# Block-product FFN: modulation columns shifted by half a step, first block step reordered

## The chip, the cores and the metric

The kernel runs on one core of a Trainium2 chip. The metric is the device time of one execution in microseconds. A core has TensorE (PE), VectorE (DVE), ScalarE (ACT) and GpSimd (POOL), which run their own instruction streams and meet at semaphores; SyncE (SP) issues all DMA transfers, in one queue.

## The reference

The program is a two-layer trunk on 1024 latent tokens of 1024 channels and a context of 256. Layer 0 has a recurrent mixer, layer 1 a pooling mixer; each is followed by a gated feed-forward block, and every sub-layer is normalised, modulated and gated by six vectors per layer, computed from the condition `c`.

```python
mod_l = jnp.split((sc @ ada_w[i] + ada_b[i])[:, None, :], N_MOD, axis=-1)   # sc = silu(c)
...
def _conv_ffn(h, w_up, conv_w, conv_b, w_down):
    z = h @ w_up.astype(h.dtype)
    u, v = z[..., :D_FF], z[..., D_FF:]
    u = _dwconv(u, conv_w, conv_b, (FFN_CONV // 2, FFN_CONV // 2))   # width 3 along the tokens
    return (jax.nn.gelu(u) * v) @ w_down.astype(h.dtype)
```

## The kernel before

Everything is channel-major: 8 tiles of 128 channels (KT), tokens along the free dimension, in two halves of 512. A float32 product is made of three fp32r products: each operand is split into a rounded part `_hi` (ScalarE, a copy) and a rest `_lo` (GpSimd or VectorE, a subtraction), and hi*hi, hi*lo and lo*hi are summed in PSUM.

**A feed-forward block** (`ffn(L)` on each engine, L = 0 and 1) has 24 steps j (FJ), one for each 128 of the 3072 hidden channels. Step 0 is made as two plain products (`first_pair`, weights "A" and "B") while the input arrives. From step 1 the up projection of u and v (two outputs, two token halves, eight channel tiles) is made of seven "quarters" of 12 products each, in the order 11, 12, S4, S1, S2, S3, 22 (`quarter`), a block scheme with fewer products than the eight plain ones. On the weight side S1, S2, S3 and S4 are combinations of weight halves, made by GpSimd (`combine`, L1317), rounded by ScalarE (`round_op`, L882) and completed by GpSimd (`lo_of_op`, L1330, So_lo, WA_lo and WB_lo). On the token side the operands are sums and differences of the halves of the input, T_raw[0] to T_raw[3], made once a block by VectorE (`right_raws`), rounded by ScalarE (`round_t`) and completed by VectorE (`right_lo`) and, for the last, GpSimd. S1 reads T[0], S2 T[1], S3 T[2] and 22 T[3]; 11, 12 and S4 read the input itself.

VectorE turns the quarters into Ub (u, by adds L1854, L1866, L1869) and V (L1863 and L1871 make U2, then L1873, L1877). ScalarE and VectorE do the convolution (`tap` L1055, `taps` L1815 and L1820), ScalarE GeLU (L1060), VectorE the gating S[1] = S[0] * V (`gated`, L1832), ScalarE F_hi (L1094), GpSimd F_lo (L1350). The down projection (`down`, L461, 8 tiles m, 48 products, weights "C" with WC_lo L1187) of step j-1 follows the quarters of step j; VectorE adds each tile to Y (`add_down`, L1744; the first time a copy, L1742). Tiles of `down` take turns on three bank pairs (4, 0, 6). Steps 2 to 22 are a hardware loop; step 23 and the last down product (`down_last`) are written out, with the sums of squares of the next norm among its adds.

**Modulation columns.** The columns of layer 1 are made beside block 0. Each step handles units e = 2j and 2j+1: a 512 KB weight unit is loaded to E (`load_unit`; one buffer, so a load waits until the sum before it is done), GpSimd multiplies it with silu(c) (`ada_product`, L1222), VectorE sums over the channel tiles (`ada_sum`, L1479), TensorE sums over partitions with products of one column (`ada_columns`, L494), VectorE adds the bias (`add_ada_bias`, L1502). Units 0 and 1 are loaded at the end of the out-projection's loads; their products come before the next stream on GpSimd and their sums in the first step of the block. In a step both sums come ahead of the U2 add, the columns after 22 and the bias add behind the taps; tile m = 1 of `down` waits for that add, since it writes bank 0, where the columns are.

**Order.** The order on each engine is written out by hand; every wait is for the semaphores named in the code. In the first step of a block TensorE does all seven quarters, then down(0).

Of the kernel before, what the change touches and what calls it, by code (L numbers as in the profile page):

```python
# [23 lines left out]
KT = D // P  # L24
# [44 lines left out]
def build_trunk(nc, xT, ctxT, params, ada, wA, wB, wC, gatew, poolw, poolcnt, ident_in, outT):  # L69
    with ExitStack() as top:  # L70
# [91 lines left out]
        READY_FIRST = ("S1", "11", "12", "S4", "S2", "S3", "22")  # L162
# [145 lines left out]
        def _(sp_):  # L308
# [147 lines left out]
        def _(pe):  # L456
# [183 lines left out]
            def down(L, j):  # L640
# [5 lines left out]
                for m in range(KT):  # L646
                    if m < 2:
                        if not first:
                            pe.wait_ge(d_added, 8 * c + m - 1)
                        if m == 1 and L == 0:  # L650
                            pe.wait_ge(ada_added, NH + 3 + j)
# [4 lines left out]
                    b = (4, 0, 6)[m % 3]  # L656
# [3 lines left out]
            def down_last(L):  # L660
# [29 lines left out]

# [23 lines left out]
            def ffn_step(L, j):  # L714
# [13 lines left out]
                quarter("S2", t, first)  # L728
                if first and L == 0:
                    pe.wait_ge(u_evac, 1)  # L730
# [4 lines left out]
                pe.wait_ge(up_added, added_at("u0", t))  # L735
                quarter("S3", t, first)
                pe.wait_ge(up_added, added_at("u2", t))
                quarter("22", t, first)
                if L == 0:
                    if first:  # L740
                        pe.wait_ge(ada_added, NH + 2)
                    else:
# [104 lines left out]
        def _(act):  # L847
# [220 lines left out]
            def ffn_first(L):  # L1068

                round_t(L, 0)  # L1070
                round_op("S1", L, 1)
                round_op("11", L, 1)
                round_op("12", L, 1)
# [5 lines left out]
                round_op("S4", L, 1)  # L1079
                round_t(L, 2)  # L1080
                round_t(L, 1)
                round_op("S2", L, 1)
                round_op("S3", L, 1)
                round_op("22", L, 1)
                round_t(L, 3)
                copy_p1(UP * L + 1)
                gelu(L, 0)

            def ffn_step(L, j):
# [3 lines left out]
                act.wait_ge(f_mul, t)  # L1093
                A(F_hi[:], S[1][:], ACT.Copy).then_inc(f_hi, 1)  # L1094
                if not first:
                    copy_p1(t)
                if not (first and L == 0):
                    round_down(L, j - 1)
# [77 lines left out]
            norm_root(5, 1)  # L1176
            next_stream(5, 2, lambda h: fill_ffn(1, h))
# [3 lines left out]
        def _(pool):  # L1181
# [51 lines left out]

            def next_stream(q, i, lo):
# [12 lines left out]
                if lo:  # L1247
                    lo(1)
# [52 lines left out]
            def combine(name, L, j):  # L1301


                t, n = UP * L + j, N_STD + FJ * L + j
                A1, A2, B1, B2 = (raw[s][:, hs(h)] for s in "AB" for h in range(2))
                S1_, S2_, S4_ = (So_raw[:, i * HF:i * HF + HF] for i in range(3))
                dst, a, b, op, before = {
                    "S1": (S1_, B1, B2, ALU.add, None), "S2": (S2_, S1_, A1, ALU.subtract, "S1"),
                    "S3": (B1, A1, B1, ALU.subtract, "S1"), "S4": (S4_, A2, S2_, ALU.subtract, "S2")}[name]
                if before is None:  # L1310
                    pool.wait_ge(raw_full["B"], 16 * n + 16)
                    pool.wait_ge(raw_full["A"], 16 * n + 16)
                else:
                    pool.wait_ge(made, made_at(before, t))
                if name != "S3" and not (isinstance(t, int) and t == 1):
                    pool.wait_ge(op_done, done_at(name, t - 1))
                TT(dst, a, b, op).then_inc(made, 1)  # L1317
# [14 lines left out]
            def ffn_first(L):  # L1332

                for name in ("S1", "S2", "S3", "S4"):
                    combine(name, L, 1)
                for name in ("S1", "11", "12", "S4", "S2", "S3", "22"):
                    lo_of_op(name, L, 1)
                for k in range(KT // 2):
# [4 lines left out]
            def ffn_step(L, j):  # L1343
                t = UP * L + j
                static = isinstance(j, int)
                first, last = static and j == 1, static and j == FJ - 1
                if L == 0:
                    ada_product(2 * j)
                pool.wait_ge(f_hi, t)
                TT((F_lo_last if last else F_lo)[:], S[1][:], F_hi[:].bitcast(F32), ALU.subtract)\  # L1350
                    .then_inc(f_ready, 1)
                if not (first and L == 0):
                    lo_of_unit("C", t - 1)
                if last:
                    if L == 0:
# [647 lines left out]
```

## Time and profile before

| | us |
|---|---|
| median of 3 runs | 2371.55 (2368.89 to 2373.41) |
| the profiled execution, its own time | 2371.26 |
| its span, first to last instruction | 2369.5 |
| mean granted TensorE clock | 0.946 |
| block 0, steps 3 to 22 (20 steps) | 728.14 |
| block 1, steps 2 to 22 (21 steps) | 646.12 |

In the trace, times are microseconds from the span's start. A product of 512 columns starts 0.23 us after the one before it when TensorE runs freely; its own duration is longer, since products are pipelined. The granted clock is a share of 2.4 GHz.

### The profile page before, as it was taken

To read this page: it belongs to the slowest core of one execution; us is meant where nothing else is said; L and a number is where in the kernel's file an instruction comes from. 1 tells how busy PE (TensorE), PEld (TensorE's weight loads), DVE (VectorE), ACT (ScalarE), POOL (GpSimd) and SP (SyncE) were. 2 spreads that over 40 slices of the span, in tenths; PEclk is the share of its full clock that TensorE was granted. 3 is DMA by queue.
4 is the path that set the end of the run, shared out by engine and by line. 5 is a ranking of instruction groups with operands and counts; after the bars stand their busy time and mean duration, and the time that the engine had idled before them with its cause. 6 is when DMAs were issued, how large, how long until landed. Compare 5 with 4: busy or idle time off the path is not lost.

```text
span 2369.5 us, 26733 instructions
## 1 busy us (share of the span) xinstructions
PE 2113.4 (89%) x9040; PEld 1692.5 (71%) x9040; DVE 1545.9 (65%) x1535; ACT 812.2 (34%) x1072; POOL 1342.9 (57%) x836
## 2 busy tenths in 40 slices
PE   7899997955889899899898997967999999999996
PEld 7677775844667677677676776855888888888885
DVE  6688885188656656656656568488665555556667
ACT  3557655244222222222222234453222222222222
POOL 1423323366575766765756736257666666666663
PEclk9999998967999999999999997978999999999998
DMA  6133221221222122222121240021111111111113
GB/s 261 71 104 110 77 101 71 80 98 36 73 69 78 63 71 80 69 73 79 63 80 62 71 151 27 19 80 45 53 45 53 44 53 53 48 50 53 53 44 142
DMA packets 52120, 174.91 MB, mean 74 GB/s; under 512 B 4817, under 2 KB 5105, under 8 KB 50929
## 3 DMA queue, kind: packets, MB, share of 16 engines
q1 hardware_dynamic: 52080, 174.41, 21.0%
q8 instruction: 22, 0.36, 0.1%
q14 instruction: 18, 0.14, 0.0%
HBM read 161.80 MB, written 12.58 MB: 74 GB/s over the span
## 4 chain that ended last, share of the span: by engine, by line
PE 48%; issue 18%; POOL 15%; DVE 10%; ACT 7%; DMA 2%; POOLq 0%; SPq 0%; ACTq 0%; DVEq 0%
PE ps L461 21%; PE ps L709 18%; PE ps L593 3%; POOL F_lo L1350 2%; POOL WC_lo L1187 2%; POOL E L1222 2%; POOL WA_lo L1330 2%; POOL So_raw L1317 2%; POOL So_lo L1330 2%; DMA E<-ada 2%; DVE T_lo L1809 1%; PE ps L821 1%; POOL WB_lo L1330 1%; DVE V L1439 1%; PE ps L500 1%
## 5 line engine op out<-in xcount | busy, mean ns | idle before, releaser
L1744 DVE TENSOR_TENSOR Y<-Y,ps 128x1024 f32<-128x1024 f32 x336 | 401.4, 1217 | 45.8 <-PE ps L461 24.2
L461 PE MATMUL ps<-F_hi,WC_hi 128*128 128x512 f32 x736 | 242.7, 408 | 39.7 <-DVE M L1502 36.1
L1330 POOL TENSOR_TENSOR So_lo<-So_raw,So_hi 128x512 fp32r<-128x512 f32 x138 | 262.8, 1930 | 11.4 <-ACT So_hi L882 11.4
L1479 DVE TENSOR_REDUCE red<-E 128x128 f32<-128x1024 f32 x47 | 92.9, 1977 | 250.9 <-POOL E L1222 250.9
L1222 POOL TENSOR_TENSOR E<-E,silu_c 128x1024 f32<-128x1024 f32 x47 | 89.6, 1906 | 281.1 <-DMA E<-ada 281.1
L461 PE MATMUL ps<-F_hi,WC_lo 128*128 128x512 f32 x736 | 233.8, 396 | 0.0
L461 PE MATMUL ps<-F_lo,WC_hi 128*128 128x512 f32 x704 | 222.2, 397 | 0.0
L882 ACT ACTIVATE So_hi<-So_raw 128x512 fp32r<-128x512 f32 x138 | 81.6, 620 | 393.5 <-POOL So_raw L1317 393.5
L1094 ACT ACTIVATE F_hi<-S 128x1024 fp32r<-128x1024 f32 x46 | 48.8, 1060 | 464.8 <-DVE S L1832 454.2
L1350 POOL TENSOR_TENSOR F_lo<-S,F_hi 128x1024 fp32r<-128x1024 f32 x44 | 105.9, 2406 | 175.8 <-ACT F_hi L1094 175.8
L461 PEld LDWEIGHTS ps<-F_hi,WC_hi 128*128 128x128 f32 x736 | 137.0, 193 | 82.5 <-DVE M L1502 45.5
L461 PEld LDWEIGHTS ps<-F_hi,WC_lo 128*128 128x128 f32 x736 | 140.8, 191 | 31.1
L709 PE MATMUL ps<-H_hi,WA_hi 128*128 128x512 f32 x368 | 148.0, 402 | 11.3 <-POOL WA_lo L1330 11.3
L461 PEld LDWEIGHTS ps<-F_lo,WC_hi 128*128 128x128 f32 x704 | 135.1, 192 | 29.9
L709 PE MATMUL ps<-T_hi,So_hi 128*128 128x512 f32 x368 | 146.0, 397 | 1.7 <-DVE T_lo L1809 1.7
L709 PE MATMUL ps<-H_lo,WA_hi 128*128 128x512 f32 x368 | 147.4, 401 | 0.0
L709 PE MATMUL ps<-H_hi,WA_lo 128*128 128x512 f32 x368 | 147.2, 400 | 0.0
L709 PE MATMUL ps<-T_lo,So_hi 128*128 128x512 f32 x368 | 145.6, 396 | 0.0
L709 PE MATMUL ps<-T_hi,So_lo 128*128 128x512 f32 x368 | 145.5, 395 | 0.0
L1863 DVE TENSOR_TENSOR U<-t,ps 128x512 f32<-128x512 f32 x46 | 31.4, 683 | 169.6 <-PE ps L709 169.6
L709 PE MATMUL ps<-H_hi,WB_hi 128*128 128x512 f32 x184 | 80.4, 437 | 45.9 <-DVE U L1863 45.9
L1330 POOL TENSOR_TENSOR WA_lo<-rawA,WA_hi 128x512 fp32r<-128x512 f32 x92 | 118.9, 1314 | 0.0
(269 smaller groups left out, 5352.4 us busy)
## 6 DMA issues: line engine op xcount, KB each, us to landing
rawA<-wA SPq DMA_DIRECT2D x60, 512.0 KB, 3.3
rawB<-wB SPq DMA_DIRECT2D x60, 512.0 KB, 3.3
E<-ada SPq DMA_DIRECT2D x47, 512.0 KB, 3.8
rawC<-wC SPq DMA_DIRECT2D x46, 512.0 KB, 3.3
quad<-ada SPq DMA_DIRECT2D x8, 2048.0 KB, 9.5
ada_first<-ada SPq DMA_DIRECT2D x4, 2048.0 KB, 16.4
outT<-X SPq DMA_DIRECT2D x16, 512.0 KB, 2.8
X<-outT SPq DMA_DIRECT2D x16, 512.0 KB, 6.8
```

Of the source, the lines that this page charges most:

```text
L461: mm = pe.matmul(out, w[:, w_cols:w_cols + P], (hi, lo)[part], start=first and w is W_hi[s] and part == 0, stop=last and w is W_lo[s])
L593: mm = pe.matmul(out, gw[:, gi], src, start=True, stop=True)
L709: mm = pe.matmul(ps[:, OUT[name]], w[:, at + k * P:at + k * P + P], right[part][:, k], start=k == 0 and w is hi and part == 0, stop=k == K ...
L882: A(dst[:, at:at + HF], src[:, src_at:src_at + HF], ACT.Copy).then_inc(op_hi, 1)
L1094: A(F_hi[:], S[1][:], ACT.Copy).then_inc(f_hi, 1)
L1187: TT(W_lo[s][:], raw[s][:], W_hi[s][:].bitcast(F32), ALU.subtract).then_inc(w_ready[s], 1)
L1222: TT(dst[:], dst[:], silu_c[:, :, 0:1].to_broadcast([P, KT, P]), ALU.mult).then_inc(e_mul, 1)
L1317: TT(dst, a, b, op).then_inc(made, 1)
L1330: TT(lo[:, at:at + HF], src, hi[:, at:at + HF].bitcast(F32), ALU.subtract).then_inc(op_ready, 1)
L1350: TT((F_lo_last if last else F_lo)[:], S[1][:], F_hi[:].bitcast(F32), ALU.subtract)\
L1479: dve.tensor_reduce(red[:, i], src[:].rearrange("p k m -> p m k"), mybir.AxisListType.X, ALU.add)\
L1744: TT(Y[:, m], Y[:, m], flat(ps[:, b:b + 2, :]), ALU.add).then_inc(d_added, 1)
```

## The change

The columns' stages are shifted by half a step: the second sum of a pair is made at the start of the next step, TensorE makes the columns between 12 and S4 of that step, and the bias add follows the first Ub add. On GpSimd F_lo is put before the first column product and the combinations before the second. Units 0 and 1 are loaded, multiplied and summed in the out-projection; the last pair's second sum, columns and coefficients go into the last down product's adds. In the first step of both blocks the weight combinations are made earlier (in `next_stream`), S4 is completed first, and down(0) comes right after S4, on two bank pairs instead of three; VectorE does the taps and the gating of step 0 between the T_raw's. For block 1 the first down weight is completed before the stream that leads to the block.

```diff
-        READY_FIRST = ("S1", "11", "12", "S4", "S2", "S3", "22")
+        READY_FIRST = ("S4", "S1", "11", "12", "S2", "S3", "22")
@@ SyncE: the out-projection's loads
+                if i == 3:
+                    load_unit(0)
+                    load_unit(1)
                 load_raw("A", NH + 2 + i)
                 load_raw("B", NH + 2 + i)
-            load_unit(0)
-            load_unit(1)
@@ TensorE: down
-                        if m == 1 and L == 0:
-                            pe.wait_ge(ada_added, NH + 3 + j)
+                        if m == 1 and L == 0 and not first:
+                            pe.wait_ge(ada_added, NH + 2 + j)
+                    elif first:
+                        pe.wait_ge(d_added, 8 * c + m - 1)
...
-                    b = (4, 0, 6)[m % 3]
+                    b = (4, 0)[m % 2] if first else (4, 0, 6)[m % 3]
@@ TensorE: down_last
-                        pe.wait_ge(ada_added, NH + 1 + FJ)
+                        pe.wait_ge(ada_added, NH + FJ)
...
+                    if n == 7 and L == 0:
+                        ada_columns(4 * NH + 2 * FJ, 2, ps[:, 3, 0:2])
@@ TensorE: ffn_step
                 if not first:
+                    if L == 0:
+                        pe.wait_ge(d_added, 8 * (c - 1))
+                        pe.wait_ge(ada_added, NH + j)
+                        ada_columns(4 * NH + 2 * j, 2, ps[:, 0, 0:2])
                     pe.wait_ge(d_added, 8 * c - 10)
                 quarter("S4", t, first)
+                if first:
+                    down(L, 0)
                 quarter("S1", t, first)
...
-                        pe.wait_ge(d_added, 8 * (c - 1))
-                    ada_columns(4 * NH + 2 * j + 2, 2, ps[:, 0, 0:2])
-                if not last:
+                if not first and not last:
                     down(L, j - 1)
@@ ScalarE: ffn_first
-                round_t(L, 0)
+                round_op("S4", L, 1)
                 round_op("S1", L, 1)
                 round_op("11", L, 1)
-                round_op("12", L, 1)
                 A(Ub[:, 1:T + 1], flat(AB01), ACT.Copy).then_inc(u_evac, 1)
                 tap(L, 0)
-                round_op("S4", L, 1)
-                round_t(L, 2)
-                round_t(L, 1)
+                round_op("12", L, 1)
                 round_op("S2", L, 1)
+                round_t(L, 0)
                 round_op("S3", L, 1)
                 round_op("22", L, 1)
+                gelu(L, 0)
+                round_t(L, 2)
+                copy_p1(UP * L + 1)
+                act.wait_ge(f_mul, UP * L + 1)
+                A(F_hi[:], S[1][:], ACT.Copy).then_inc(f_hi, 1)
+                round_t(L, 1)
                 round_t(L, 3)
-                copy_p1(UP * L + 1)
-                gelu(L, 0)
@@ ScalarE, before the second block's stream
+            round_down(1, 0)
             next_stream(5, 2, lambda h: fill_ffn(1, h))
@@ GpSimd: next_stream
                 if lo:
+                    for name in MADE_ORDER:
+                        combine(name, q // 4, 1)
                     lo(1)
@@ GpSimd: the out-projection
             for m in range(KT):
+                if m == 6:
+                    ada_product(0)
                 lo_of_unit("AB"[m % 2], NH + m // 2 + 1)
+                if m == 6:
+                    ada_product(1)
@@ GpSimd: ffn_first and ffn_step
-                for name in ("S1", "S2", "S3", "S4"):
-                    combine(name, L, 1)
+                for name in READY_FIRST:
                     lo_of_op(name, L, 1)
+                pool.wait_ge(f_hi, UP * L + 1)
+                TT(F_lo[:], S[1][:], F_hi[:].bitcast(F32), ALU.subtract).then_inc(f_ready, 1)
...
+                if not first:
+                    pool.wait_ge(f_hi, t)
+                    TT((F_lo_last if last else F_lo)[:], ...).then_inc(f_ready, 1)
                 if L == 0:
                     ada_product(2 * j)
...
                 lo_of_op("12", L, j + 1)
+                for name in MADE_ORDER:
+                    combine(name, L, j + 1)
                 if L == 0:
                     ada_product(2 * j + 1)
-                for name in ("S1", "S2", "S3", "S4"):
-                    combine(name, L, j + 1)
@@ GpSimd, before the second block's stream
+            lo_of_unit("C", UP)
             next_stream(5, 2, lambda h: fill_ffn(1, h))
@@ VectorE: even_sums_whole (the out-projection's squares)
+                for i in range(2):
+                    ada_sum(0, i)
@@ VectorE: add_down_last
+                    if n == 3 and L == 0:
+                        ada_sum(FJ - 1, 1)
+                    if n == 9 and L == 0:
+                        later_coefs()
@@ VectorE: right_raws (T_raw[0], T_raw[2], T_raw[1], T_raw[3] in this order)
-                right_lo(L, 0)                       # was behind T_raw[0]
+                taps(L, 0)                           # behind T_raw[2]
+                gated(L, 0)                          # behind T_raw[1]
@@ VectorE: ffn_first
                 right_raws(L)
+                right_lo(L, 0)
+                add_down(L, 0)
                 right_lo(L, 1)
-                taps(L, 0)
                 right_lo(L, 2)
-                if L == 0:
-                    ada_sum(0, 0)
-                    ada_sum(0, 1)
@@ VectorE: ffn_step
-                gated(L, j - 1)
-                if L == 0 and not first:
-                    ada_sum(j, 0)
+                if not first:
+                    if L == 0:
+                        ada_sum(j - 1, 1)
+                    gated(L, j - 1)
                 TT(u_0, t1[:], p["12"], ALU.add).then_inc(up_added, 1)
...
+                if L == 0 and not first:
+                    add_ada_bias(ps[:, 0, 0:2], 46 + 2 * j, 2, NH + 1 + j)
+                    ada_sum(j, 0)
...
+                if first:
+                    v_first_half()
+                    taps(L, j)
+                    if L == 0:
+                        ...
+                        add_ada_bias(ps[:, 0, 0:2], 48, 2, NH + 2)
+                        ada_sum(1, 0)
+                    return
```

## Rows read from the trace of the kernel before

**Rows 1.** The page, busy time by engine (share of the span) and instructions.
```profile
PE 2113.4 (89%) x9040; PEld 1692.5 (71%) x9040; DVE 1545.9 (65%) x1535; ACT 812.2 (34%) x1072; POOL 1342.9 (57%) x836
```
**Rows 2.** Busy time by stretches, the loops: us; busy by engine; clock, DMA, GB/s.
```profile
647.89:1376.03 728.14, 653.64 (x2722) 518.81 (x2721) 454.75 (x421) 173.78 (x240) 483.81 (x300) 0.96 0.21 71
1653.20:2299.32 646.12, 646.12 (x2773) 518.95 (x2772) 394.14 (x379) 182.19 (x252) 433.11 (x273) 1.00 0.15 50
```
**Rows 3.** TensorE's waits from 647.9 to 1376: total us, times, longest.
```profile
PE ps L709 <- DVE U L1863: 41.8, 20, 2.7
PE ps L461 <- DVE M L1502: 32.7, 20, 2.3
```
**Rows 4.** Timeline of TensorE, the columns: start, us, what.
```profile
816.06 0.50 PE L494 MATMUL ps<-ones,red 128*128 128x1 f32 x4
```
**Rows 5.** Timeline of VectorE, a step of block 1.
```profile
2300.89 1.22 DVE L1832 TENSOR_TENSOR S<-S,V 128x1024 f32<-128x1024 f32 x1
2305.35 0.69 DVE L1854 TENSOR_TENSOR Ub<-t,ps 128x512 f32<-128x512 f32 x1 [3.24 <-PE ps L709]
2313.75 0.69 DVE L1863 TENSOR_TENSOR U<-t,ps 128x512 f32<-128x512 f32 x1 [7.71 <-PE ps L709]
```
**Rows 6.** Timeline of GpSimd and VectorE, a step of block 0.
```profile
799.57 1.91 POOL L1222 TENSOR_TENSOR E<-E,silu_c 128x1024 f32<-128x1024 f32 x1 [11.86 <-DMA E<-ada]
801.44 2.41 POOL L1350 TENSOR_TENSOR F_lo<-S,F_hi 128x1024 fp32r<-128x1024 f32 x1
806.15 2.55 POOL L1330 TENSOR_TENSOR WA_lo<-rawA,WA_hi 128x512 fp32r<-128x512 f32 x2
810.52 1.27 POOL L1317 TENSOR_TENSOR So_raw<-rawB 128x512 f32<-128x512 f32 x1
810.60 1.91 DVE L1479 TENSOR_REDUCE red<-E 128x128 f32<-128x1024 f32 x1 [6.45 <-POOL E L1222]
815.68 5.72 POOL L1330 TENSOR_TENSOR So_lo<-So_raw,So_hi 128x512 fp32r<-128x512 f32 x3
```
**Rows 7.** The page, a costly group (busy, mean ns) and transfers (us to landing).
```profile
L1094 ACT ACTIVATE F_hi<-S 128x1024 fp32r<-128x1024 f32 x46 | 48.8, 1060 | 464.8 <-DVE S L1832 454.2
...
E<-ada SPq DMA_DIRECT2D x47, 512.0 KB, 3.8
rawC<-wC SPq DMA_DIRECT2D x46, 512.0 KB, 3.3
```
**Rows 8.** Timeline of TensorE, first steps; in brackets the idle time before.
```profile
546.70 0.79 PE L709 MATMUL ps<-H_hi,WA_hi 128*128 128x512 f32 x1 [5.54 <-POOL WA_lo L1330]
...
598.31 0.99 PE L494 MATMUL ps<-ones,red 128*128 128x1 f32 x4 [10.62 <-DVE red L1479]
...
1602.36 0.77 PE L709 MATMUL ps<-H_hi,WA_hi 128*128 128x512 f32 x1 [5.75 <-POOL WA_lo L1330]
```
**Rows 9.** Timeline of VectorE, first step of block 0.
```profile
540.41 6.79 DVE L1809 TENSOR_TENSOR T_lo<-T_raw,T_hi 128x512 fp32r<-128x512 f32 x4
563.64 2.30 DVE L1815 SCALAR_TENSOR_TENSOR S<-Ub,par,S 128x1024 f32<-128x1024 f32 x1
602.10 1.23 DVE L1742 COPY Y<-ps 128x1024 f32<-128x1024 f32 x1 [2.61 <-PE ps L461]
```
**Rows 10.** Timeline of GpSimd, ahead of block 0.
```profile
480.90 1.90 POOL L1222 TENSOR_TENSOR E<-E,silu_c 128x1024 f32<-128x1024 f32 x1 [1.60 <-DMA E<-ada]
482.76 2.35 POOL L1222 TENSOR_TENSOR E_first<-E_first,silu_c 128x1024 f32<-128x1024 f32 x1
```
**Rows 11.** Timeline of SyncE and VectorE, ahead of block 1.
```profile
1539.09 0.33 SPq L446 DMA_DIRECT2D rawC<-wC  x1
1545.51 1.57 DVE L1439 TENSOR_TENSOR V<-V 128x512 f32<-128x512 f32 x1
1551.68 0.69 DVE L1445 TENSOR_TENSOR V<-V,acc 128x512 f32<-128x512 f32 x1
```
**Rows 12.** Timeline of TensorE, start of the last down product of block 0.
```profile
1399.13 0.50 PE L461 MATMUL ps<-F_hi,WC_hi 128*128 128x512 f32 x1 [1.02 <-DVE M L1502]
```

More of the change, by code:

```diff
@@ L1092, in ffn_step @@
                 first, last = static and j == 1, static and j == FJ - 1
-                act.wait_ge(f_mul, t)
-                A(F_hi[:], S[1][:], ACT.Copy).then_inc(f_hi, 1)
                 if not first:
+                    act.wait_ge(f_mul, t)
+                    A(F_hi[:], S[1][:], ACT.Copy).then_inc(f_hi, 1)
                     copy_p1(t)
-                if not (first and L == 0):
                     round_down(L, j - 1)
@@ L1232, in add_odd, with combine @@
                     TT(X[:, m, hs(h)], X[:, m, hs(h)], Y[:, m, hs(h)], ALU.add).then_inc(x_new[1], 1)
+            def combine(name, L, j):
+                t, n = UP * L + j, N_STD + FJ * L + j
+                A1, A2, B1, B2 = (raw[s][:, hs(h)] for s in "AB" for h in range(2))
+                S1_, S2_, S4_ = (So_raw[:, i * HF:i * HF + HF] for i in range(3))
+                dst, a, b, op, before = {
+                    "S1": (S1_, B1, B2, ALU.add, None), "S2": (S2_, S1_, A1, ALU.subtract, "S1"),
+                    "S3": (B1, A1, B1, ALU.subtract, "S1"), "S4": (S4_, A2, S2_, ALU.subtract, "S2")}[name]
+                if before is None:
+                    pool.wait_ge(raw_full["B"], 16 * n + 16)
+                    pool.wait_ge(raw_full["A"], 16 * n + 16)
+                else:
+                    pool.wait_ge(made, made_at(before, t))
+                if name != "S3" and not (isinstance(t, int) and t == 1):
+                    pool.wait_ge(op_done, done_at(name, t - 1))
+                TT(dst, a, b, op).then_inc(made, 1)
             def next_stream(q, i, lo):
@@ L1299, in _ @@
             lo_of_unit("C", 0)
[L1301 to L1317, printed above, removed]
             def lo_of_op(name, L, j):
@@ L1346, in ffn_step @@
                 first, last = static and j == 1, static and j == FJ - 1
+                if not first:
+                    pool.wait_ge(f_hi, t)
+                    TT((F_lo_last if last else F_lo)[:], S[1][:], F_hi[:].bitcast(F32), ALU.subtract)\
+                        .then_inc(f_ready, 1)
                 if L == 0:
                     ada_product(2 * j)
[L1349 to L1352, printed above, removed]
+                if not first:
                     lo_of_unit("C", t - 1)
                 if last:
-                    if L == 0:
-                        ada_product(2 * j + 1)
                     pool.wait_ge(lastw_hi, L + 1)
@@ L1739, in add_down @@
                     dve.wait_ge(d_done, 8 * (FJ * L + j) + m + 1)
-                    b = (4, 0, 6)[m % 3]
+                    b = (4, 0)[m % 2] if isinstance(j, int) and j == 0 else (4, 0, 6)[m % 3]
                     if isinstance(j, int) and j == 0:
@@ L1744, in add_down, with later_coefs @@
                         TT(Y[:, m], Y[:, m], flat(ps[:, b:b + 2, :]), ALU.add).then_inc(d_added, 1)
+            def later_coefs():
+                add_ada_bias(ps[:, 3, 0:2], 46 + 2 * FJ, 2, NH + 1 + FJ)
+                dve.wait_ge(ada_added, NH + 1 + FJ)
+                coefs(2, 1, 0)
+                coefs(3, 1, 1)
+                shift_steps(1)
+                gates(2, 1, 0)
+                gates(3, 1, 1).then_inc(coef_ready, 1)
+                dve.wait_ge(coef_ready, 3)
+                dve.wait_ge(cols_step, 1)
+                TS(cc[:, 2], cc[:, 1], ROUNDER, None, ALU.add).then_inc(cols_step, 1)
+                dve.wait_ge(cols_step, 2)
+                TS(cc[:, 0], cc[:, 2], -ROUNDER, -1.0, ALU.add, ALU.mult).then_inc(cols_ready, 1)
             def add_down_last(L):
@@ L1826, in gated @@
                 if isinstance(j, int) and j == 0:
-                    dve.wait_ge(unit_done["B"], N_STD + L + 1)
+                    for s in "AB":
+                        dve.wait_ge(unit_done[s], N_STD + L + 1)
                     TT(S[1][:], S[0][:], flat(AB45), ALU.mult).then_inc(f_mul, 1)
```

50 lines of the change are left out of this document (12 added, 38 removed).

## The prediction

> **What bounds the kernel now.** I read the page first: TensorE is busy for 89% of the span and nothing else passes 65% [rows 1]. So only stretches in which TensorE stands still or runs slowly can give time back. Second, the busy time by stretches, cut at the first product of a step [rows 2]. The two feed-forward blocks run the same 132 large products per step, and only the first also makes the modulation columns of the next layer. Its 20 steps from 647.89 to 1376.03 take 728.14 us, 36.41 each; the second block's 21 steps take 646.12 us, 30.77 each. The second has no TensorE idle time and a granted clock of 1.00 (2.4 GHz throughout), the first 0.96. Third, TensorE's waits in the first block's loop [rows 3]: 41.8 us before the product "22" for the add that makes U2, and 32.7 us before the down product for the add of the modulation bias. That is 3.73 us a step, for one small side computation. Its chain is: column unit by DMA, product on GpSimd (L1222), sum on VectorE (L1479), four one-column products (L494), bias add (L1502).
>
> Step excess: 36.41 - 30.77 = 5.64 us, of which 3.73 waiting and at most 0.50 for the four one-column products, a row of whose group lasts 0.50 us [rows 4]; I take 0.36, since they overlap their neighbours. The rest, 1.55 us, is the clock: stretches at 1.2 GHz follow some of the waits.
>
> **The loop after the change (first block, steps 3 to 22).** The second sum of a pair moves to the start of the next VectorE step, the columns go between "12" and "S4", the bias add follows the first Ub add, and on GpSimd F_lo comes before the first product and the combinations before the second. The question is whether the shifted chain now fits. I lay it on the second block's step, T being TensorE's first product: there the last down tile is added and gating starts at T+1.6, the Ub add is at T+6.0 and the U2 add at T+14.4, after 7.71 us of waiting for TensorE [rows 5], with T = 2299.32, where the second stretch of [rows 2] ends.
> - VectorE: sum of the second column unit T+1.5 to 3.4 (1.91 us [rows 6]), gating (1.22) to 4.7; F_hi 1.06 us [rows 7] to 5.8; F_lo on GpSimd (2.41) to 8.3.
> - TensorE finishes "12" at T+5.6 (24 products at 646.12/(21 x 132) = 0.233 us [rows 2]) and then needs that sum: 2.2 us of slack.
> - The next column load goes out at about T+3.6 and takes 3.8 us [rows 7], so it is there at 7.4, before F_lo ends. GpSimd: product 8.3 to 10.2, WC_lo (the size of F_lo) to 12.6, WA_lo (2.55) to 15.1, four combinations (1.27 each) to 20.5, second product to 22.4, three So_lo (5.72) to 28.1, two WB_lo (the size of WA_lo) to 30.7 [rows 6]. "S4" needs the three only at T+31+6, so GpSimd has 9 us of slack.
> - VectorE's first sum waits for the product at 10.2 and ends at 12.2; the U2 add can start at 14.8. Slack 2.6 us, where now the sum is late and TensorE waits.
> No wait is left, so the clock should stay at 1.00 as in the second block. A step costs 30.77 + 0.36 = 31.13: 20 x (36.41 - 31.13) = **-105.6 us**. Bounds: no gain from the clock, -74; four small products free, -113.
>
> **First steps of the first block.** TensorE now waits 5.54 us for WA_lo (the combinations stand before it on GpSimd), and 10.62 us for the second of two column sums, with the first of much the same length [rows 8]. The first pair ends at 546.70 - 5.54 = 541.2; step 3 starts at 647.9. New order, all prices from rows of this stretch [rows 9] or the loop:
> - Combinations are done earlier; GpSimd rounds S4, S1, 11 in turn (1.7 us each beside VectorE): "11" starts at 541.7; 11, 12, S4 run to 550.1.
> - VectorE: T_raw0 to 540.4 (as now, the 6.79 us row starts there), T_raw2 (four at 1.7) to 547.2, two taps (2.3 and 1.7) to 551.1, T_raw1 to 553.7 (four of about 0.65 once GpSimd is idle), gating to 554.9. F_hi to 556.0, F_lo to 558.5. down(0) starts 8.5 us after S4, its first products at half clock.
> - T_raw3, then right_lo(0) (four at 1.7, beside GpSimd) to 564.1; only then the copies of down(0), 1.23 us each, with two bank pairs: its third tile waits for the first copy, and it ends near 575.
> - S1, S2 follow; "S3" waits for the Ub add behind right_lo(1) and right_lo(2) (eight of 0.69 us alone [rows 11]); step 2 starts at 589.5.
> - New wait: the sum of unit 2 stands at the very end of VectorE's step 1 (594.5), unit 3 is loaded only after it (product 599 to 601), and behind that product on GpSimd stand the So_lo of step 2. "S4" of step 2 can start at about 606.5 instead of 595.5: 11 us of idle and 1.7 us of slow clock. Queued behind unit 3 on SyncE are the B and C weights of the next steps; by the same count they arrive some 5 us before they are needed.
> Step 2 then runs with about 2 us of small waits; step 3 starts at 635: 635 - 647.9 = **-13**. Bounds: -26 if the new wait is hidden, 0 if VectorE's operations take their contended times throughout.
>
> **Second block's first step.** First pair ends 1602.36 - 5.75 = 1596.6 [rows 8], step 2 starts at 1653.2: 56.6 us. The new order without column work takes 48: **-8.6** (bounds 0 and -12).
>
> **Before the blocks.** Ahead of the first block, the two column products (480.90 to 485.1) leave GpSimd, where the additions to X wait behind them [rows 10]; VectorE then shares less with GpSimd. Bounds 0 and -4.2; I take **-2.5**. The sums move to 465-469, before a merge that TensorE wants at 471.4: if their load is 2 us late, +2. Ahead of the second block, GpSimd's WC_lo is put in front of the X additions. Its weight is issued at 1539.09 [rows 11] and takes 3.3 us [rows 7], rounding the 1.06 of F_hi, WC_lo the 2.41 of F_lo: GpSimd comes free for its additions to X only at 1546.2. The fourth-square sum, now at 1545.5 to 1547.1, moves to about 1550-1551.5, and the merge at 1551.68 by some 4.5: **+4.5** (bounds 0 and +7). The combinations now lie beside the merge of both streams: a VectorE add of 128x512 took 0.69 us alone and 1.57 beside a GpSimd operation [rows 11], so +0.7 each, **+1.4**.
> The Trainium skill (SBUF — State Buffer, "SBUF: two separate sides") says that a VectorE operation with two SBUF inputs and a GpSimd operation lock each other out for a whole instruction. By that rule each merge could wait a full combination, estimated from the 1.27 us row: +2.5 for both instead of +1.4. The 1.57 us row agrees in kind with the rule.
>
> **The end of the first block.** The bias wait of 1.02 us before the last down product goes [rows 12]; one sum (1.9) and the later coefficients (about 1) enter VectorE's last adds. Tile sums at TensorE's eleventh half tile may come 1 us later: **+0.5** net, bounds -1 and +4.
>
> **Sum.** -105.6 - 13 - 8.6 - 2.5 + 4.5 + 1.4 + 0.5 = -123.3. The profiled execution took 2371.26 us for a span of 2369.5; the median of the runs is 2371.55. So 2371.3 - 123.3 = **2248 us**.
>
> **Rivals.**
> A. The chain doesn't quite fit: one of the two waits stays in every step. For it: the slack at the U2 add is 2.6 us and hangs on the load landing before F_lo ends; GpSimd's waits for these loads are up to 11.86 us now [rows 6]. Against it: that wait is now behind the late second sum, which moves forward. Price: 2.09 us and half of the 1.55 us of clock, 20 x 2.9 = 58: 2306 us.
> B. Slower: the late unit 3 of step 1 never gets caught up. Each load waits for a sum, each sum for a product, and VectorE is held before gating in every step. It decides once the sum that TensorE needs at T+5.6 comes over 5.3 us late, the present step's excess over 31.1; were it 11 us late, as in step 2, a step would be 42: 20 x 5.7 = 114 more than now, near 2470 even with the smaller losses and gains. Against it: the ring of two loads, products and sums takes about 16 us of a 31 us step, so it recovers in one step.
> C. The new first step brings nothing: down(0) waits for VectorE as long as the column sums did. Price: 13 + 8.6: 2270 us.
> D. The loop does as forecast and the first block's new 11 us wait is hidden: 2236 us.
>
> **Chances.** Forecast 0.70 (its own range 2240 to 2260), A 0.12, B 0.03, C 0.09, D 0.06. The range 2234 to 2280 leaves out A, B and a little more. A measurement of this kernel can't tell less than 0.2% (5 us) from no change. Faster 0.95 (all but B and mishaps I don't see), same 0.02, slower 0.03.
>
> **What would show it.** In the profile of the changed kernel: the first block's loop at 31.1 us a step, clock 1.00 and no TensorE wait on the U2 or bias add (A: one of them stays; B: the wait before "S4" is in every step). One wait of about 11 us before "S4" in step 2, released by So_lo; none in the second block. A gap of 8 to 9 us before down(0) in both. The first pair of the second block starting 4 to 6 us later after the pooling stage than now. The prediction is wrong if the loop step is over 32 us, or if the two first steps together gain under 5 us.

## The result and the profile after

The changed kernel takes 2282.5 us (median of 4 runs, 2281.5 to 2283.2), the kernel before 2370.2 us (2367.5 to 2373.4): ratio 0.963, 95% interval 0.961 to 0.965. Faster, as forecast, but 34.5 us above the 2248 forecast and 2.5 us beyond the range. The profiled execution has a span of 2281.5 us for 2369.5 before. The 88.0 us by stages, from TensorE's instructions:

| stage | before | after | difference | forecast |
|---|---|---|---|---|
| start to end of block 0's first pair | 541.2 | 539.3 | -1.9 | -1.8 |
| block 0, steps 1 and 2 | 106.7 | 100.5 | -6.3 | -13 |
| block 0, steps 3 to 22 | 728.1 | 641.4 | -86.8 | -105.6 |
| end of block 0, pooling, block 1's first pair | 220.6 | 226.7 | +6.1 | +5.7 |
| block 1, steps 1 and 2 | 87.4 | 88.2 | +0.8 | -8.6 |
| rest | 685.5 | 685.6 | 0 | 0 |

So three lines missed, by 18.8, 6.7 and 9.4 us, all to the same side; their sum, 34.9 us, is the miss. Without the first of them the time would lie inside the range. The loops by stretches, then TensorE's waits in block 0's loop (total us, times, longest), where [rows 3] had 41.8 and 32.7 us:

```profile
639.71:1281.07 641.36, 624.74 (x2721) 503.21 (x2720) 472.33 (x421) 173.26 (x240) 486.11 (x300) 1.00 0.25 81
1595.95:2211.20 615.25, 615.25 (x2641) 494.23 (x2640) 375.30 (x361) 173.35 (x240) 412.71 (x260) 1.00 0.15 50
```
```profile
PE ps L462 <- DVE Y L1758: 16.6, 20, 0.8
```

Both old waits are gone and the clock is back at 1.00 (2.4 GHz), against 0.96 in [rows 2]. A step takes 641.36/20 = 32.07 us, 1.30 above block 1's. Of this 0.83 is a new wait, in each step, before the fourth down tile, for VectorE's first add to Y; the other 0.47 are the four column products: TensorE's busy time is 31.24 us a step for 30.76, at a granted clock of 1.00 in both. VectorE's groups in the two loops after (busy, mean ns of one), block 0 first:

```profile
L1852 DVE SCALAR_TENSOR_TENSOR S<-Ub,par,S 128x1024 f32<-128x1024 f32 x20 | 46.5, 2325 | 0.0
L1847 DVE SCALAR_TENSOR_TENSOR S<-Ub,par,S 128x1024 f32<-128x1024 f32 x20 | 46.4, 2318 | 0.0
```
```profile
L1847 DVE SCALAR_TENSOR_TENSOR S<-Ub,par,S 128x1024 f32<-128x1024 f32 x20 | 41.4, 2070 | 0.0
L1852 DVE SCALAR_TENSOR_TENSOR S<-Ub,par,S 128x1024 f32<-128x1024 f32 x20 | 34.3, 1717 | 0.0
```

The two taps, which stand directly before the adds, take 4.64 us together in block 0 and 3.79 in block 1. One step of VectorE and GpSimd shows why:

```profile
1107.70 2.33 DVE L1847 SCALAR_TENSOR_TENSOR S<-Ub,par,S 128x1024 f32<-128x1024 f32 x1
...
1110.56 2.32 DVE L1852 SCALAR_TENSOR_TENSOR S<-Ub,par,S 128x1024 f32<-128x1024 f32 x1
1112.80 2.34 DVE L1758 TENSOR_TENSOR Y<-Y,ps 128x1024 f32<-128x1024 f32 x2
```
```profile
1107.63 1.32 POOL L1256 TENSOR_TENSOR So_raw<-rawA,So_raw 128x512 f32<-128x512 f32 x1
1108.88 2.92 POOL L1228 TENSOR_TENSOR E<-E,silu_c 128x1024 f32<-128x1024 f32 x1
```

The second column product, moved behind the combinations, now lies beside the second tap. Alone a tap takes 1.28 us (1561.12, below) and the product 1.91 [rows 6]. Here they take turns: the tap comes up at 1110.56, the product goes on to 1111.8, and some 1.1 us later, at 1112.9, the tap ends. The product in turn lost 1 us to the first tap. The Trainium skill (SBUF — State Buffer, "Who interferes with whom") says just this of a VectorE instruction with two SBUF inputs and a GpSimd one that reads SBUF; the trace agrees, within 0.2 us (1111.8 and 1.28 make 1113.1, the tap ends at 1112.9).

TensorE's waits in the first steps, block 0 (539 to 640), then block 1 (1507 to 1600):

```profile
PE ps L462 <- POOL F_lo L1349: 9.1, 1, 9.1
PE ps L495 <- DVE red L1493: 6.1, 1, 6.1
PE ps L713 <- DVE Ub L1886: 4.4, 1, 4.4
PE ps L462 <- DVE Y L1758: 3.5, 1, 3.5
PE ps L713 <- POOL So_lo L1342: 1.7, 1, 1.7
PE ps L462 <- DVE Y L1756: 1.2, 1, 1.2
```
```profile
PE ps L462 <- POOL F_lo L1349: 9.0, 1, 9.0
PE ps L713 <- DVE Ub L1886: 4.3, 1, 4.3
PE ps L462 <- DVE Y L1758: 2.6, 1, 2.6
PE ps L462 <- DVE Y L1756: 2.1, 1, 2.1
```

The 9 us for F_lo were forecast. So was the late column sum, as 11 us before S4; it shows as 6.1 us before the columns and 1.7 before S4. The Ub add before S3 was named in the prediction, with less time; of the waits for Y in step 2 it had "about 2 us of small waits" in block 0 and nothing in block 1. Behind these waits, in block 1, on VectorE, ScalarE and SyncE:

```profile
1544.30 8.12 DVE L1841 TENSOR_TENSOR T_lo<-T_raw,T_hi 128x512 fp32r<-128x512 f32 x8
1552.34 0.68 DVE L1886 TENSOR_TENSOR Ub<-t,ps 128x512 f32<-128x512 f32 x1
...
1561.12 1.28 DVE L1847 SCALAR_TENSOR_TENSOR S<-Ub,par,S 128x1024 f32<-128x1024 f32 x1
```
```profile
1573.08 1.06 ACT L867 ACTIVATE WC_hi<-rawC 128x1024 fp32r<-128x1024 f32 x1 [5.22 <-DMA rawC<-wC]
```
```profile
1567.46 0.33 SPq L404 DMA_DIRECT2D rawB<-wB  x1
1568.13 0.34 SPq L409 DMA_DIRECT2D rawC<-wC  x1
```

VectorE reaches the Ub add only after eight T_lo subtractions, which stand behind the copies of down(0). In step 2 the C weight is asked for behind the B weight of the step after, and ScalarE waits for it with all its later work queued behind. Ahead of block 1, last, TensorE waits 9.2 us, where it waited 3.9, for the fourth of the squares (S, L900, made by ScalarE from X) that the norm sums; WC_lo on GpSimd delays the additions to X:

```profile
1459.37 1.87 PE L501 MATMUL ps<-ones,S 128*128 128x1 f32 x8 [9.21 <-ACT S L900]
```
```profile
1448.84 2.35 POOL L1193 TENSOR_TENSOR WC_lo<-rawC,WC_hi 128x1024 fp32r<-128x1024 f32 x1 [10.45 <-ACT WC_hi L867]
```

### The profile page after: what moved, and what is told of

It is laid out like the page before. It is cut to its first block, busy times and chain, and to the rows that moved or that the text cites. A ratio compares the mean times of both kernels' runs of the same rounds, so it can differ in the third digit from the quotient of the medians.

```text
span 2281.5 us, 26751 instructions
## 1 busy us (share of the span) xinstructions
PE 2086.4 (91%) x9040; PEld 1677.3 (74%) x9040; DVE 1565.5 (69%) x1535; ACT 809.9 (35%) x1072; POOL 1343.6 (59%) x836
## 4 chain that ended last, share of the span: by engine, by line
PE 67%; DVE 15%; ACT 8%; issue 7%; POOL 2%; ACTq 0%; DVEq 0%; DMA 0%; POOLq 0%
PE ps L713 32%; PE ps L462 26%; PE ps L594 3%; DVE S L1847 2%; PE ps L825 1%; ACT S L1059 1%; DVE V L1451 1%; DVE Y L1758 1%; PE ps L501 1%; DVE T_lo L1841 1%; ACT TH L988 1%; DVE Y L1538 1%; PE ps L537 1%; DVE T_raw L1807 1%; PE ps L792 1%
## 5 line engine op out<-in xcount | busy, mean ns | idle before, releaser
L1758 DVE TENSOR_TENSOR Y<-Y,ps 128x1024 f32<-128x1024 f32 x336 | 393.3, 1213 | 14.1 <-PE ps L462 2.2
L1361 POOL TENSOR_TENSOR F_lo<-S,F_hi 128x1024 fp32r<-128x1024 f32 x42 | 101.2, 2409 | 314.4 <-ACT F_hi L1101 314.4
L1342 POOL TENSOR_TENSOR So_lo<-So_raw,So_hi 128x512 fp32r<-128x512 f32 x138 | 238.4, 1755 | 2.2 <-ACT So_hi L886 2.2
L1101 ACT ACTIVATE F_hi<-S 128x1024 fp32r<-128x1024 f32 x44 | 46.7, 1061 | 435.9 <-DVE S L1865 435.9
L1228 POOL TENSOR_TENSOR E<-E,silu_c 128x1024 f32<-128x1024 f32 x47 | 110.7, 2355 | 26.9 <-DMA E<-ada 26.9
L1342 POOL TENSOR_TENSOR WB_lo<-rawB,WB_hi 128x512 fp32r<-128x512 f32 x92 | 119.8, 1323 | 4.6 <-ACT WB_hi L886 4.6
L1193 POOL TENSOR_TENSOR WC_lo<-rawC,WC_hi 128x1024 fp32r<-128x1024 f32 x46 | 110.8, 2410 | 15.4 <-ACT WC_hi L867 15.4
```

The source lines that it names most:

```text
L1193: TT(W_lo[s][:], raw[s][:], W_hi[s][:].bitcast(F32), ALU.subtract).then_inc(w_ready[s], 1)
L1228: TT(dst[:], dst[:], silu_c[:, :, 0:1].to_broadcast([P, KT, P]), ALU.mult).then_inc(e_mul, 1)
L1342: TT(lo[:, at:at + HF], src, hi[:, at:at + HF].bitcast(F32), ALU.subtract).then_inc(op_ready, 1)
L1758: TT(Y[:, m], Y[:, m], flat(ps[:, b:b + 2, :]), ALU.add).then_inc(d_added, 1)
```

## The experiments

All are edits of the changed kernel. Ratios are to the kernel before, run beside them; the changed kernel's own is 0.963 (0.961 to 0.965).

| kernel | median, us | ratio (95%) | span | span against 2281.5 |
|---|---|---|---|---|
| product_late | 2263.3 | 0.957 (0.955 to 0.959) | 2260.2 | -21.3 |
| product_early | 2303.8 | 0.974 (0.972 to 0.975) | 2303.8 | +22.3 |
| copies_act | 2266.1 | 0.958 (0.956 to 0.960) | 2263.9 | -17.6 |
| wc_behind | 2278.1 | 0.963 (0.961 to 0.965) | 2276.4 | -5.1 |
| second_first_undone | 2278.6 | 0.961 (0.959 to 0.962) | 2278.2 | -3.3 |
| unit2_early | 2277.2 | 0.960 (0.959 to 0.962) | 2275.8 | -5.7 |
| rawc_first | 2276.5 | 0.960 (0.959 to 0.962) | 2273.2 | -8.3 |
| best | 2236.8 | 0.943 (0.942 to 0.945) | 2234.7 | -46.8 |
| best_taps | 2235.7 | 0.943 (0.942 to 0.945) | 2234.8 | -46.7 |
| best_both | 2231.1 | 0.941 (0.940 to 0.943) | 2231.2 | -50.3 |
| best_mix | 2230.4 | 0.941 (0.939 to 0.942) | 2227.1 | -54.4 |

The intervals of wc_behind, second_first_undone, unit2_early and rawc_first overlap that of the changed kernel. What is said of these four below rests on the stages of their traces, one execution each.

**The product beside the taps.** Two moves of the same instruction, one to either side.

```diff
-                if L == 0:
-                    ada_product(2 * j + 1)
                 for name in READY_ORDER[2:]:
                     lo_of_op(name, L, j + 1)
+                    if name == "S4" and L == 0:
+                        ada_product(2 * j + 1)
```


> The changed kernel with one move on GpSimd: in the steps of the first block the second column product (L1228, 2.9 us) comes after the three So_lo, not before them. Theory: the 0.83 us wait for the first Y add in each of the 20 loop steps comes from the product lying beside VectorE's second tap (2.32 us there, 1.72 us in the second block, where short So_lo subtractions lie beside it). Then the taps take 2.06 and 1.72 us, the wait goes and a loop step falls from 32.07 to about 31.2 us: -16 to -18 us, plus up to 1.7 us in step 2, where So_lo no longer stands behind the late product: 2264 us. Rival: the adds are late because of VectorE's own order (a sum and a bias add more than in the second block) or because of the four column products; then the step stays at 32.0 to 32.1 and only step 2 changes: 2281 us.

```diff
+                if L == 0 and not first:
+                    ada_product(2 * j + 1)
                 for name in MADE_ORDER:
                     combine(name, L, j + 1)
-                if L == 0:
+                if L == 0 and first:
                     ada_product(2 * j + 1)
```


> The changed kernel with the second column product of the loop steps (steps 2 to 22 of the first block) back ahead of the four combinations on GpSimd, where the kernel before has it. Theory: its column unit is asked for only after the first sum, so the product can't start before about 1104.7 in the step where the combinations now start at 1103.65; they follow it at about 1106.7, ScalarE rounds S1 before its tap and waits for the first of them, so VectorE's taps start 2.2 us later and the adds too: the wait before the fourth down tile grows from 0.8 to about 3 us, step 34.3, some +40 us: 2325 us. Rival (place of the product is of no weight, only VectorE's own order): 2282 us. Second rival (contention alone counts and the combinations are cheaper beside the taps than the product is): 2265 us.

Loop waits of TensorE and groups of VectorE, with the product late, then with it early:

```profile
PE ps L462 <- DVE Y L1758: 4.1, 20, 0.3
```
```profile
L1847 DVE SCALAR_TENSOR_TENSOR S<-Ub,par,S 128x1024 f32<-128x1024 f32 x20 | 46.2, 2308 | 0.0
L1852 DVE SCALAR_TENSOR_TENSOR S<-Ub,par,S 128x1024 f32<-128x1024 f32 x20 | 34.2, 1711 | 0.0
```
```profile
PE ps L462 <- DVE Y L1760: 32.6, 20, 1.8
```
```profile
L1849 DVE SCALAR_TENSOR_TENSOR S<-Ub,par,S 128x1024 f32<-128x1024 f32 x20 | 36.9, 1844 | 36.0 <-ACT S L1059 36.0
L1854 DVE SCALAR_TENSOR_TENSOR S<-Ub,par,S 128x1024 f32<-128x1024 f32 x20 | 34.3, 1715 | 0.0
```

| | taps and the idle before them | wait | step |
|---|---|---|---|
| block 1 | 3.79 | 0 | 30.8 |
| product late | 4.02 | 0.20 | 31.4 |
| changed kernel | 4.64 | 0.83 | 32.1 |
| product early | 3.56 + 1.80 | 1.63 | 32.9 |

Each time the wait is what the taps take over 3.8 us. That settles the loop: the chain had no room at this place, and the product beside the second tap took 0.63 us of it; 0.2 remains, since the first tap still meets a combination. The rival (VectorE's own order) would have left 0.83. Early, the taps are indeed quicker, but ScalarE's tap is late behind the rounding of S1, as expected; at 1.63 us rather than 3 the price was about half of that expected. Late, step 2 of block 0 also fell, from 48.5 to 41.9 us, more than the 1.7 forecast: the wait for So_lo went, that for Y fell to 2.2, and the clock of the step rose from 0.86 to 0.92. The span fell by 21.3 us, of which 12.6 are the loop's and 6.6 step 2's. But 4.0 more are in block 1's steps 1 and 2, which the edit does not touch (last section); by the ratios the move is worth some 14 us.

**The copies of down(0).** On ScalarE, after it rounds the next 11 and 12:

```diff
+                    if first:
+                        for m in range(KT):
+                            act.wait_ge(d_done, 8 * FJ * L + m + 1)
+                            b = (4, 0)[m % 2]
+                            A(Y[:, m], flat(ps[:, b:b + 2, :]), ACT.Copy).then_inc(d_added, 1)
...
                 right_lo(L, 0)                  # VectorE
-                add_down(L, 0)
```


> The changed kernel with the eight copies of the first down product (L1756, 1.23 us each on VectorE) made by ScalarE, which stands idle there, in both blocks. Theory: in the first step VectorE is the engine that is full, from the first T_raw to the Ub add, and with 10 us less of work the 2.07 and 1.20 us waits of the down product for its copies and the 4.35 us wait before S3 go, with the slow clock behind them: 6 to 9 us in each block, 2282 - 15 = 2267 us. Rival: the waits come from the order in which GpSimd and ScalarE deliver the parts, and VectorE only stands last; then the waits move to another releaser and the time stays within 4 us: 2280 us. Where the first block's step 2 then waits longer for its late column unit, half of its share is lost.

The first step falls from 51.5 and 53.0 us to 43.3 in both blocks. The waits for Ub and for the copies are gone; in block 1's steps 1 and 2 (1499 to 1578) TensorE waits for F_lo in the first, for Y in the second and for So_lo in between:

```profile
PE ps L462 <- POOL F_lo L1354: 9.0, 1, 9.0
PE ps L462 <- DVE Y L1763: 3.6, 1, 3.6
PE ps L713 <- POOL So_lo L1347: 0.9, 1, 0.9
```

The first step was full on VectorE; the rival falls. Nearly all of the gain stays; block 1's step 2 pays 1.0 us back.

**WC_lo of block 1.** Its rounding and subtraction back into the first step:

```diff
-            round_down(1, 0)          # ScalarE, and lo_of_unit("C", UP) on GpSimd
...
+                if L:                 # ScalarE, before gelu(L, 0)
+                    round_down(L, 0)
...
+                if L:                 # GpSimd, before F_lo
+                    lo_of_unit("C", UP)
```


> The changed kernel with the second block's first WC_lo (and its rounding on ScalarE) back behind the stream: in the first step, ahead of F_lo, where GpSimd stands idle 7.2 us. Theory: the 9.22 us wait for the fourth square ahead of the second block falls back to 3.9 us as in the kernel before, and WC_lo is hidden in the first step: -5 us, 2277 us. Rival: VectorE's T_raw and tap operations beside it take their contended times longer and F_lo is later, so most of it is paid back before the first down product: 2281 us.

The stage ahead of block 1 falls by 4.8 us, and the wait for the square is 3.88 as before. But F_lo comes 2 us later:

```profile
1522.88 1.19 PE L462 MATMUL ps<-F_hi,WC_hi 128*128 128x512 f32 x2 [10.97 <-POOL F_lo L1352]
```

Against the changed kernel the ratio shows nothing. The traces show 3 us (4.8 less 2), which is no more than two executions can differ by, and 2 more that are the wait and the clock of step 2 (last section). The forecast's +4.5 for this term is right, and the idle 7 us of GpSimd in the first step were not free for it: beside the tap WC_lo took 3.3 us and the tap 3.3.

**The second block's reordering undone.** PE, ScalarE, GpSimd and VectorE run the first step of L = 1 as the kernel before does, WC_lo and the combinations included:

```diff
-                if first:
+                if first and L == 0:
                     down(L, 0)
...
-                if not first and not last:
+                if (not first or L) and not last:
                     down(L, j - 1)
```


> The changed kernel with the second block's first step, its WC_lo and its combinations put back in the order of the kernel before; the first block stays changed. Theory: in the second block the new order of the first step brings nothing in sum (steps 1 and 2 took 87.4 us before and 88.2 after), and WC_lo and the combinations ahead of it cost 6.1 us, so undoing both gains about 7 us: 2275.5 us. Rival (the forecast's: the new first step is worth 8.6 us and something else took it back, later or by chance): undoing it loses 8.6 and gains 6.1: 2285 us.

From step 23 of block 0 to step 3 of block 1 it takes 308.9 us for 314.9 in the changed kernel: 6.0 of the 7 expected, and the theory holds. TensorE waits 5.6 us for WA_lo again, as in [rows 8], and for the fourth square 3.9 instead of 9.2: the early combinations and WC_lo had only moved a wait from one side of the first pair to the other, and the new order of the first step gave nothing (from the end of the first pair to step 3, 87.6 us for 88.4). The span shows 3.3 us of it, since steps 1 and 2 of block 0, which are not changed, took 102.7 us for 100.1 in this execution.

**The sum of unit 2.** The counts and columns of units 0 and 1 follow TensorE's S2, and on VectorE the bias add and `ada_sum(1, 0)` follow the second Ub add, not the taps:

```diff
                 quarter("S2", t, first)
+                if first and L == 0:
+                    pe.wait_ge(d_added, 8)
...
+                    ada_columns(4 * NH + 2, 2, ps[:, 0, 0:2])
```


> The changed kernel with one move in the first step of the first block: the counts and the columns of units 0 and 1 come after TensorE's S2, not after 22, and the sum of unit 2 comes on VectorE after the second Ub add, not after the taps. So unit 3 is asked for some 12 us earlier. Theory: the waits of step 2 for the sum of unit 3 (6.11 us before the four column products, 1.71 us before S4) are the price of the late sum of unit 2 and go, with the slow clock behind them: -8 to -10 us, 2273 us. Rival: with them gone, step 2 is held by its late weights and taps (the wait of 3.47 us before a down tile grows), and half comes back: 2278 us.

Step 2 of block 0 falls from 48.5 to 40.4 us; its wait for the sum is 0.6 us instead of 6.1. A new wait of 4.4 us stands before 22, for the U2 add, which VectorE makes only behind the first sum of the step; that sum's unit is asked for behind the late B and C weights. In `best`, where the C weight has moved too, this wait is gone. The median, 2277.2, is nearer to the rival's 2278 than to the theory's 2273; the whole moves by 5.7 us only, since block 0 begins 1.4 us later and block 1's stages are 1 us longer in this execution.

**The C weight of step 2.** Its request moves ahead of those of step 3's A and B:

```diff
-                if not (isinstance(j, int) and j == 1):
+                if not (isinstance(j, int) and j <= 2):
                     load_down(L, j - 1)
                 if L == 0:
                     load_unit(2 * j)
+                if isinstance(j, int) and j == 1:
+                    load_down(L, 1)
+                if L == 0:
                     load_unit(2 * j + 1)
```


> The changed kernel with one move on SyncE, in both blocks: the C weight of step 2 is asked for ahead of the A and B weights of step 3, not behind them. Theory: ScalarE's rounding of it (5.22 us of waiting in the second block's step 2) stands in front of the rounding of WA, GpSimd's WC_lo, WA_lo and combinations and so of the tap; with the weight there in time the taps of step 2 start 2.5 us earlier and the waits of 2.57 and 3.47 us for Y adds in step 2 of the two blocks go, with the slow clock behind them: -4 to -8 us, 2276 us. Rival: raw B of the same step is as late and holds the combinations, so the taps stay late: 2281 us.

ScalarE waits for it no more; step 2 falls from 48.5 to 43.5 us in block 0 and from 34.8 to 30.6 in block 1. The theory holds, at 8 us by the trace.

**Together.** `best` has product_late, copies_act, unit2_early and rawc_first.

> Four moves together on the changed kernel: the second column product behind the three So_lo, the copies of down(0) on ScalarE, the C weight of step 2 asked for first, the sum of unit 2 early. Theory: they take away different waits and add up but for step 2 of the first block, where three of them meet: -14 (loop and what it brings elsewhere) -16 (copies) -4 (C weight) -4 (rest of step 2): 2244 us. Rival: in the first blocks' steps 1 and 2 one wait takes the place of another, and beside the first move only half of the rest is left: 2256 us.

2236.8 us, 7 less than expected: little of the four gains overlaps (together 46.8 us of span, one by one 52.9). Block 0's steps 1 and 2 take 44.1 + 33.9 us (51.5 + 48.5), block 1's 43.1 + 30.6, the loop 31.4 a step. What is left in step 1 is F_lo's 9 us. One more order puts the taps and the gating before the T_raw of S3, S2 and 22, and on ScalarE F_hi before their rounding:

```diff
                     minus(T_raw[0][:, k], Y[:, k, hs(1)], Y[:, k, hs(0)]).then_inc(t_raw, 1)
+                taps(L, 0)
+                gated(L, 0)
                 dve.wait_ge(x_saved[1], 64 * (L + 1))
```


> The four moves and one more, in the first step of both blocks: VectorE makes the two taps and the gating before T_raw of S3, S2 and 22, not after eight of them, and ScalarE makes F_hi before it rounds these. Theory: the 9.1 us wait before down(0) is VectorE's order (T_raw operations of 1.78 us beside GpSimd stand in front of the taps), and since the copies of down(0) no longer load VectorE, it has the T parts ready in time: the wait falls to about 2 us, -6 to -7 us a block, 2237 - 13 = 2224 us. Rival: VectorE is still nearly full, and S1, S2 or S3 wait for T_lo by as much as down(0) gained: 2234 us.

The wait changed its place. Step 1 takes 42.8 us for 44.1 in block 0 and 43.1 for 43.1 in block 1, and block 0's step 2 takes 1.7 us more. TensorE in block 0:

```profile
551.19 0.70 PE L466 MATMUL ps<-F_hi,WC_hi 128*128 128x512 f32 x2 [2.49 <-POOL F_lo L1358]
...
559.92 1.22 PE L466 MATMUL ps<-F_hi,WC_hi 128*128 128x512 f32 x2 [4.43 <-ACT Y L1115]
```

The theory is a miss: the time is the rival's, though not by VectorE. The 4.4 us are for ScalarE's first copy of down(0), which by the code stands behind its roundings and writes over Y, from which the T_raw are made. Two more, the second on top of the first:

```diff
                     pool.memset(Ub[:, T + 1:T + 2], 0.0)
+                    if L:                      # best_both
+                        lo_of_unit("C", UP)
...
                 round_t(L, 1)
+                copy_down(L, (0, 1))           # best_mix: copies among the roundings
                 round_t(L, 3)
+                copy_down(L, (2, 3))
```


> As the kernel with the taps first, and the second block's first WC_lo on GpSimd stands behind its additions to X, in the 4.4 us in which it waits for the first H_hi, not ahead of them. Theory: the 9.3 us wait for the fourth square before the second block falls to 3.9 us and WC_lo costs nothing elsewhere: -5 us against the run beside it, 2219 us. Rival: it stands in front of the first H_lo and of the X addition that the second half needs, and 2 to 3 us come back: 2222 us.

> As the last kernel, with ScalarE's copies of down(0) put among its roundings: the first two as soon as the T parts that read these tiles are made, not behind the rounding of the last T part and of two weights. Theory: in the last kernel the wait moved, from F_lo (9.1 us, now 1.8) to the first copy (5.7 us, ScalarE busy with roundings until then); about 3.5 us of it and the slow clock behind it go, in both blocks: -7 to -9 us, 2223 us. Rival: VectorE's T_lo and GpSimd's H_lo come later by the copies' time, and S2, S3 or 22 wait instead: 2230 us.

With WC_lo behind the additions the wait for the square is 4.4 us instead of 9.4, and the total falls by 4.6 us for 5 expected. The copies among the roundings gain 3.1 us of step 1 in block 1 (42.2 to 39.1) and lose 2.7 in block 0 (43.0 to 45.7), where TensorE now waits 5.3 us for the Ub add; step 2 gives 2.5 of them back. The medians show no difference (runs from 2227.0 to 2232.8 us), and 2230.4 is the rival's time. The best version is 2231 us, some 0.978 of the changed kernel by the two ratios (0.9414 to 0.9629).

## Why the prediction was right and wrong

- **The bound, and the two waits of the loop.** Right: both waits went and the clock returned. 86.8 of 105.6 us came. By its own sign ("wrong if the loop step is over 32 us") the prediction fails all the same, at 32.07.
- **The step that failed: "No wait is left, so the clock should stay at 1.00 as in the second block. A step costs 30.77 + 0.36 = 31.13".** The clock part held; a wait was left, which the sum put at nothing. I had laid only the columns' own chain on block 1's step, and asked for each place whether GpSimd and VectorE are in time, not what they do to each other there. The second product lands at T+20 (T, TensorE's first product, is 1088.9 in the step above), near the T+20.5 of the prediction; that is beside the second tap, and the adds that follow have no slack. That wait is 16.6 us; the columns at 0.47 instead of 0.36 are 2.2. Together 18.8, all of the loop's miss. Both moves of the product show it.
- **First steps of block 0.** The gap before down(0) came, 9.1 us for 8.5, and the chain of unit 3 ends as forecast: S4 of step 2 starts at 606.1, for 606.5. Most of that wait (6.1 of 7.8 us) is released by VectorE's sum before the columns, though, not by So_lo before S4. Two prices were too low. From the end of down(0) to step 2 I had 14.5 us (575 to 589.5), and it took 18.1: the eight T_lo of right_lo(1) and right_lo(2) stood at 0.69 us, though the combinations lie beside them (8.12 us for the eight), and the wait before S3 is 4.35 us. And from S4 of step 2 to step 3, where I had "about 2 us of small waits", I had 28.5 us and it took 33.6: the waits are 4.4 us, and TensorE needs 29.2 us for 108 products that take 25.2 at the full clock. The weights B and C, which I had 5 us before they are needed, are not late for TensorE: WC_lo ends at 620.5, its first use is at 623.7. But ScalarE waits 8.45 us for the C weight, and I did not ask which engines stand in line behind it. unit2_early and rawc_first separate the two.
- **First step of block 1.** The same two, without column work: step 1 gained 3.2 of 8.6 us, and step 2, which I took as untouched, lost 4.0, the price of the C weight and the clock. copies_act and rawc_first give it back.
- **Before the blocks, end of block 0.** -1.9 and +6.1 for -1.8 and +5.7: right. The second also part by part: 5.3 for WC_lo (4.5 forecast), 0.7 for a merge (0.7), 0.1 for the end of block 0 (0.5). The larger price that the prediction names for the merges, +2.5, did not come. Its slips (four combinations from T+15.1 end at T+20.2, not 20.5; the two merge rows differ by 0.88 us, not 0.7) change nothing.
- **Rivals.** B did not happen; the ring of column units recovers in one step. A named the right kind (a chain without room at one place) at the wrong place: 0.83 us instead of 2.9. C came three quarters true: the first steps of the two blocks gained 5.5 of 21.6 us. D did not: the column sum of step 2 was not hidden.

## What to carry to other kernels

When an operation is moved on GpSimd, look at what VectorE does at the new time. Here a tap (two inputs from SBUF) and a product side by side took 2.32 and 2.92 us, for 1.28 and 1.91 alone, so that the two together cost nearly their sum; this counts where VectorE's next result is the one that TensorE waits for. A chain that has "no waits" in one loop can have no slack either; read the slack of every wait, not only of the one that is removed. In a prologue that is reordered, add up the work of each engine between two fixed points, then ask for each late load who is queued behind it.

## What was not expected of the hardware

The clock after a small wait is not the same from run to run of the same code. Here is block 1's step 2, which product_late does not change, in the changed kernel (1561.3 to 1596.2) and in product_late, with the granted clock behind the busy times:

```profile
1561.30:1596.20 34.90, 32.28 (x133) 25.86 (x134) 20.34 (x19) 10.28 (x14) 22.59 (x14) 0.95 0.18 61
```
```profile
1542.10:1574.70 32.60, 30.87 (x132) 24.76 (x133) 20.02 (x19) 10.26 (x14) 22.60 (x14) 1.00 0.17 58
```

The wait for Y was 2.6 us in one and 1.7 in the other, and only behind the longer one did TensorE run at 1.2 GHz for a while: 2.3 us in all. The same in step 1 (53.0 and 51.3). So two single executions differ by some 4 us in the first steps of one block alone, where the code is the same, and effects of 2 to 4 us there are not told apart by one trace. Why the waits themselves differ was not found.
